# Row tiles taken in turn at the stage borders of a two-block transformer kernel, with five raw and four high weight slots

## The chip, the cores and the metric

The kernel runs on one core of a Trainium2 chip. The metric is the device time of one execution in microseconds (us), the median of several runs. All arithmetic is in float32; a product of two float32 matrices is made of three matmuls on halves, as told below.

## The reference

x is 256 rows (tokens) by 1024. Two different blocks follow each other, each of two layers (DEPTH = 2). Every layer is FFN, token mixer, FFN, each added to the running h. Cut to what matters:

```python
# block 0
for l in range(2):
    h = h + 0.5 * swiglu(rms_norm(h, ffn1_norm[l]), w1[l], w3[l], w2[l])
    h = h + token_mixer(rms_norm(h, mix_norm[l]), ...)     # attention + multiscale pool, gated, @ w_out
    h = h + 0.5 * swiglu(rms_norm(h, ffn2_norm[l]), ...)
h = rms_norm(h, final_norm)
# block 1: the branch's result is normed too, before it is added
for l in range(2):
    h = h + 0.5 * rmsnorm(swiglu_2(rmsnorm(h, ffn1_pre_g[l]), ...), ffn1_post_g[l])
    h = h + rmsnorm(mixer(rmsnorm(h, mix_pre_g[l])), mix_post_g[l])   # scan + retention + attention
    h = h + 0.5 * rmsnorm(swiglu_2(rmsnorm(h, ffn2_pre_g[l]), ...), ffn2_post_g[l])
# rms_norm(x, g) = x * rsqrt(mean(x*x over the row) + 1e-6) * g
```

The hidden width of an FFN is 2816. Twelve stages in all: f1, m, f2 in each of four layers.

## The kernel before

**Tiles.** The 256 rows are two row tiles of 128 (row 0 and row 1, `r` in the code). h lies in SBUF by rows. At the entry of a stage TensorE transposes h, 16 tiles of 128x128, into PSUM banks `work`; ScalarE reads them with the gain as scale and writes the high part `xt_hi` (rounded to the fp32r type), and VectorE writes the low part `xt_lo`. The factor 1/rms of a row is not applied there: it is a number for each row, and is multiplied in behind the first product (the silu and the hidden product of an FFN read `rs`). So the matmuls of a stage can start before the norm is known.

**Weights.** All weights are read once, in units of 128x2048 (1 MB): SyncE (SP) asks for a unit (`load`, two DMAs of 512 KB into `raw`), ScalarE copies it to `w_hi` (`split`, L889), VectorE subtracts to `w_lo` (`split`, L1151), and TensorE multiplies x_hi by w_hi, x_hi by w_lo, and x_lo by w_hi (`product`, L521). A unit takes 24 matmuls, 12 for each row tile. raw, w_hi and w_lo have three slots each, and unit u lies in slot u mod 3. A load waits for `unit_split`: that VectorE is through with the raw slot three units before. ScalarE's copy waits for the load and for `unit_used`: that TensorE is through with the slot.

**An FFN** runs in 11 steps of 256 hidden columns (`steps`). A step has two gate/up units (u, u+1; 4 of the 8 k tiles each) and one down unit (u+4). Its products go to `work[2]` and `work[3]`; silu on ScalarE (L940) and the hidden product on VectorE (L1193) follow, then four transposes (`turn_hidden`), the halves `yt_hi` (ScalarE L945) and `yt_lo` (VectorE L1199), and the down product into `acc`. The gate/up products of step j+1 stand on TensorE before the down product of step j, so the chain of silu and transposes lies beside matmuls, apart from the last step, behind whose gate/up products nothing but its own down product is left.

**What sets the order.** Each engine has its own program, written out by hand, and waits on semaphores whose counts are computed by `Table`s. The steps and the layers are hardware loops (`Fori`). At a border between stages, TensorE ends the last product for both rows; VectorE adds the result to h in four pieces. In block 0 that is one operation for each piece (L1225 behind an FFN). In block 1 it is a norm first (`add_normed`): scale by the post gain from PSUM (L1236), squares on ScalarE (`squares_out`, L914), mean on VectorE (L1172, L1175), the power -1/2 on GpSimd (`power`, L488), and the addition (L1243). Then `turn_h` transposes all 16 tiles, xt_hi (L898) and xt_lo (L1162) follow in four pairs of pieces that hold both rows, and the first chunk (two units, 48 matmuls) begins. On ScalarE the order is: xt_hi of both rows, squares of h, split of unit u+2, split of u+3. On VectorE: xt_lo of both rows, mean, split of u+2 and more.

**SP's order at the border.** Units u and u+1 of the next stage, then `small`: in block 1 (and for f1) it waits for `h_ready`, all four pieces of h, then loads the post gain (and the pre gains), since the buffers of these are in use until then; only then unit u+2.

**Start and end.** x is loaded into `field` and added into h by VectorE (L1144). TensorE's first matmul makes a table of relative biases; behind its first two copies ScalarE issues a DMA that writes this table 128 times into a scratch tensor in DRAM (L922, 3 MB), which block 1 reads later with another stride. At the end one DMA writes all of h (L476).

Of the kernel before, what the change touches and what calls it, by code (L numbers as in the profile page):

```python
# [18 lines left out]
ALU = mybir.AluOpType  # L19
# [4 lines left out]
ds = bass.ds  # L24
# [3 lines left out]
SLOTS = 3  # L28
# [4 lines left out]
class Table:  # L33


    def __init__(self, n, uses):
        self.n, self.at, self.total, k = n, {}, [0] * n, 0
        for name, count in uses:
            for i in range(count):
                self.total[k % n] += 1  # L40
                self.at[name, i] = (k % n, self.total[k % n])
                k += 1
# [5 lines left out]
def tables(block, steps):  # L48

    if block == 0:  # L50
        mix_units = 21
        mix_work = [("turn_m", 4), ("pool", 2), ("qkT", 4), ("scores0", 8), ("probsT0", 8), ("mixp", 2), ("turn_o", 2),
                    ("turn_y", 4)]
        splits = [("turn_m", 4), ("mixp", 2), ("turn_o", 2), ("turn_y", 4)]
        chunks = [("q", 1), ("kv", 1), ("p", 1), ("gate", 3), ("pv0", 1), ("gate_b", 1), ("br_a", 2), ("br_p", 2)]
        norms = ["f1", "m", "f2"]
    else:
        mix_units = 57
        mix_work = [("turn_m", 4), ("rqkT", 4), ("decay", 4), ("ret", 4), ("turn_r", 4), ("qkT", 6),
                    ("scores0", 8), ("probsT0", 8), ("scores1", 8), ("probsT1", 8), ("turn_o", 4),  # L60
                    ("xbcT", 6), ("xsT", 4), ("cb", 2), ("acs", 1), ("seg", 16), ("turn_s", 4), ("turn_y", 4)]
        splits = [("turn_m", 4), ("turn_r", 4), ("turn_o", 4), ("turn_s", 4), ("turn_y", 4)]
        chunks = [("rqk", 2), ("rv", 2), ("gate_r", 2), ("rg", 2), ("aq", 2), ("akv", 1), ("br_r", 2),
                  ("gate_a0", 1), ("pv0", 1), ("gate_a1", 1), ("pv1", 1), ("br_a", 2),
                  ("xbc", 3), ("dt", 1), ("z", 2), ("gate_s", 2), ("ys", 2), ("br_s", 2)]
        norms = ["f1", "p1", "m", "s", "pm", "f2", "p2"]
    return dict(
        units=Table(SLOTS, [("all", 6 * steps + mix_units)]),
        work=Table(4, [("turn_f1", 4)] + mix_work + [("turn_f2", 4)]),
        split=Table(1, [("turn_f1", 4)] + splits + [("turn_f2", 4)]),  # L70
        chunks=Table(2, chunks),
        norms=Table(1, [(n, 1) for n in norms]),
    )


def build(nc, a):
# [7 lines left out]
    T = [tables(b, steps) for b in range(2)]  # L84
# [7 lines left out]
    with ExitStack() as ctx:  # L92
# [7 lines left out]
        raw = sb("raw", [P, SLOTS, UNIT])  # L100
        w_hi = sb("w_hi", [P, SLOTS, UNIT], F32R)
        w_lo = sb("w_lo", [P, SLOTS, UNIT], F32R)
# [16 lines left out]
        ms = sb("ms", [P, 2])  # L119
# [64 lines left out]
        raw_loaded = [sem(f"raw_loaded{s}") for s in range(SLOTS)]  # L184
# [7 lines left out]
        x_loaded = sem("x_loaded")  # L192
# [29 lines left out]
        h_ready = sem("h_ready")  # L222
        squared = sem("squared")
# [7 lines left out]
        pair_added = sem("pair_added")  # L231
# [5 lines left out]
        def count(kind, block, l, name, i=0):  # L237

            slot, k = T[block][kind].use(name, i)
            before = sum(T[b][kind].total[slot] for b in range(block)) * depth  # L240
            return slot, l * T[block][kind].total[slot] + (before + k)

        def unit_count(block, l, pos):

            slot, per, first = pos % SLOTS, T[block]["units"].total, T[0]["units"].total
            return slot, l * per[slot] + ((first[slot] * depth if block else 0) + pos // SLOTS + 1)

        def used_count(block, l, pos, r=1, j=0):

            slot, n = unit_count(block, l, pos)  # L250
            return slot, (n + j) * 2 + (r + 1)

        STAGES = 3

        def h_count(block, l, stage):

            return l * (4 * STAGES) + (4 + (4 * STAGES * depth + 4 if block else 0) + 4 * stage)

        def stage_of(block, name):
            return {"f1": 0, "m": 1, "f2": 2}[name]  # L260

        def norm_count(block, l, name):

            return count("norms", block, l, name)[1] + (1 if block else 0)

        def ffn_count(block, l, name, per):

            return l * (2 * per) + per * ((2 * depth if block else 0) + (name == "f2"))

        first_unit = {(b, "f1"): 0 for b in range(2)}  # L270
        for b in range(2):
            n = sum(T[b]["units"].total)
            first_unit[b, "m"] = 3 * steps
            first_unit[b, "f2"] = n - 3 * steps
            assert n % SLOTS == 0 and first_unit[b, "f2"] % SLOTS == 0
# [6 lines left out]
        def events(block, l, per, k):  # L282

            return l * per[block] + ((per[0] * depth if block else 0) + k)
# [15 lines left out]
        def _(sp):  # L300
            def load(block, l, pos, parts, j=0):

                slot, n = unit_count(block, l, pos)
                n = n + j
                sp.wait_ge(unit_split[slot], n)
                for dst, src in parts(raw[:, slot, :]):
# [1440 lines left out]
```

## Time and profile before

| | before |
|---|---|
| median of 3 runs | 2836.59 us (2836.15 to 2836.85) |
| span of the profiled execution | 2832.0 us |
| TensorE (PE) busy | 2651.5 us, 94% |
| VectorE (DVE) busy | 1551.1 us, 55% |
| ScalarE (ACT) busy | 1225.4 us, 43% |
| GpSimd (POOL) busy | 22.2 us, 1% |

The profiled execution is told by its span only; the 4.6 us between span and median lie around the program. TensorE is busy for 94% of the span, so its idle time, and the stretches in which its granted clock is low, are where time could be. The other engines and the DMA queues matter where TensorE waits for them. In the lines of a timeline, the number in brackets is the idle time of that engine before the instruction, followed by what ended it.

### The profile page before, as it was taken

What the parts mean: (1) busy time and instruction counts of PE and PEld (TensorE: products, weight loads), DVE (VectorE), ACT (ScalarE), POOL (GpSimd) and SP (SyncE); (2) the same over time, 40 slices, a digit from 0 to 9 for tenths busy, and PEclk for the clock granted to TensorE, in tenths of its full rate; (3) what the DMA queues carried; (4) which work ended last, traced back from release to release, by engine and by line L of the source; (5) the groups of instructions that cost most, each with busy time, mean ns of one, the idle gap of its engine ahead of it and who ended that gap; (6) DMA issues with size and microseconds to landing.
All of it is one profiled execution on the core that took longest, in us unless ns stands there. A gap on an engine that the chain in (4) does not pass through costs nothing.

```text
span 2832.0 us, 34364 instructions
## 1 busy us (share of the span) xinstructions
PE 2651.5 (94%) x12238; PEld 2207.2 (78%) x12238; DVE 1551.1 (55%) x1700; ACT 1225.4 (43%) x1431; POOL 22.2 (1%) x28
## 2 busy tenths in 40 slices
PE   6999899999999998999998998898999998998898
PEld 5888778878787787787877877787887877877786
DVE  3555654554565545445556585555445556585544
ACT  4444444444453444444444453444444444453443
POOL 0000000000000000000000000000000000000000
PEclk9999999999999999999999998999999999998999
DMA  9564345555644455655552431563654552441554
GB/s 227 180 228 163 117 151 186 170 179 188 205 149 132 165 190 177 209 189 169 187 168 75 150 134 60 186 192 130 207 188 167 188 169 75 150 134 60 186 190 136
DMA packets 311801, 460.58 MB, mean 163 GB/s; under 512 B 18144, under 2 KB 209936, under 8 KB 311440
## 3 DMA queue, kind: packets, MB, share of 16 engines
q1 hardware_dynamic: 309632, 456.05, 49.0%
q10 hardware_dynamic: 2064, 3.15, 0.9%
q8 instruction: 64, 1.05, 0.2%
q14 instruction: 41, 0.34, 0.0%
HBM read 454.94 MB, written 4.19 MB: 162 GB/s over the span
## 4 chain that ended last, share of the span: by engine, by line
issue 99%; POOL 1%; DVE 0%; DVEq 0%; POOLq 0%
POOL sm L496 0%; POOL rs L488 0%; POOL rp L488 0%; DVE h L1243 0%; DVEq L92 0%; POOLq L487 0%; POOLq L491 0%; POOL minus_half L482 0%; POOLq L495 0%; DVEq L1658 0%; POOLq L488 0%; DVEq L1240 0%; POOLq L1739 0%
## 5 line engine op out<-in xcount | busy, mean ns | idle before, releaser
L1151 DVE TENSOR_TENSOR w_lo<-raw,w_hi 128x2048 fp32r<-128x2048 f32 x422 | 966.5, 2291 | 823.6 <-ACT w_hi L889 823.1
L889 ACT CAST w_hi<-raw 128x2048 fp32r<-128x2048 f32 x422 | 804.6, 1908 | 647.8 <-PE acc L521 325.0
L521 PE MATMUL work<-w_hi,xt_hi 128*128 128x512 f32 x1408 | 562.1, 399 | 27.2 <-DVE xt_lo L1162 27.2
L521 PE MATMUL work<-w_hi,xt_lo 128*128 128x512 f32 x1408 | 553.7, 393 | 0.0
L521 PE MATMUL work<-w_lo,xt_hi 128*128 128x512 f32 x1408 | 552.9, 393 | 0.0
L521 PE MATMUL acc<-w_hi,yt_hi 128*128 128x512 f32 x1088 | 433.4, 398 | 29.9 <-DVE yt_lo L1162 18.3
L521 PE MATMUL acc<-w_lo,yt_hi 128*128 128x512 f32 x1088 | 429.7, 395 | 0.0
L521 PE MATMUL acc<-w_hi,yt_lo 128*128 128x512 f32 x1088 | 429.0, 394 | 0.0
L521 PE MATMUL acc<-w_hi,xt_hi 128*128 128x512 f32 (+2 forms) x896 | 346.7, 387 | 5.3 <-DVE field L1263 4.2
L521 PE MATMUL acc<-w_lo,xt_hi 128*128 128x512 f32 (+2 forms) x896 | 343.2, 383 | 0.0
L521 PE MATMUL acc<-w_hi,xt_lo 128*128 128x512 f32 (+2 forms) x896 | 343.1, 383 | 0.0
L521 PEld LDWEIGHTS work<-w_hi,xt_hi 128*128 128x128 f32 x1408 | 267.7, 190 | 82.9 <-DVE xt_lo L1162 29.7
L521 PEld LDWEIGHTS work<-w_hi,xt_lo 128*128 128x128 f32 x1408 | 267.0, 190 | 57.6
L521 PEld LDWEIGHTS work<-w_lo,xt_hi 128*128 128x128 f32 x1408 | 268.0, 190 | 53.8
L521 PEld LDWEIGHTS acc<-w_hi,yt_hi 128*128 128x128 f32 x1088 | 208.5, 192 | 78.2 <-DVE yt_lo L1162 20.5
L521 PEld LDWEIGHTS acc<-w_hi,yt_lo 128*128 128x128 f32 x1088 | 208.0, 191 | 44.3
L521 PEld LDWEIGHTS acc<-w_lo,yt_hi 128*128 128x128 f32 x1088 | 208.7, 192 | 42.9
L521 PEld LDWEIGHTS acc<-w_hi,xt_hi 128*128 128x128 f32 x896 | 173.5, 194 | 37.8 <-DVE field L1263 4.5
L521 PEld LDWEIGHTS acc<-w_hi,xt_lo 128*128 128x128 f32 x896 | 173.0, 193 | 32.5
L521 PEld LDWEIGHTS acc<-w_lo,xt_hi 128*128 128x128 f32 x896 | 173.4, 194 | 31.6
L940 ACT ACTIVATE field<-work,rs 128x256 f32<-128x256 f32 x176 | 83.3, 475 | 247.5 <-PE work L521 247.4
L945 ACT CAST yt_hi<-work 128x512 fp32r<-128x512 f32 x88 | 51.7, 587 | 296.6 <-PE work L529 296.6
(155 smaller groups left out, 1670.4 us busy)
## 6 DMA issues: line engine op xcount, KB each, us to landing
raw<-ffn_w_dram SPq DMA_DIRECT2D x264, 512.0 KB, 4.1
raw<-w_in_dram SPq DMA_DIRECT2D x204, 512.0 KB, 4.4
raw<-w_ffn_in_dram SPq DMA_DIRECT2D x180, 512.0 KB, 4.6
raw<-w_ffn_out_dram SPq DMA_DIRECT2D x88, 512.0 KB, 4.1
raw<-w_branch_dram SPq DMA_DIRECT2D x48, 512.0 KB, 4.7
raw<-w_out_dram SPq DMA_DIRECT2D x32, 512.0 KB, 4.5
bias<-b_gate_dram SPq DMA_DIRECT2D x10, 512.0 KB, 7.7
raw<-w_branch_attn_dram SPq DMA_DIRECT2D x8, 512.0 KB, 4.2
```

Of the source, the lines that this page charges most:

```text
L521: last = nc.tensor.matmul(out, x[:, kt, k], y[:, slot, w], start=start and n == 0, stop=stop and n == 2)
L889: nc.scalar.copy(w_hi[:, slot, :], raw[:, slot, :]).then_inc(hi_split[slot], 1)
L940: nc.scalar.activation(act_gate[:, r, :], work[2 + r][:, 0:NARROW], ACT.Silu, scale=rs[:, r:r + 1]).then_inc(silu_ready, 1)
L945: nc.scalar.copy(yt_hi[:, 0:2, :], work[0][:, :].rearrange("p (t n) -> p t n", t=2)) \
L1151: nc.vector.tensor_tensor(w_lo[:, slot, :], raw[:, slot, :], w_hi[:, slot, :].bitcast(F32), ALU.subtract).then_inc(unit_split[slot], 1)
```

## The change

- **Slots.** `raw` and `w_lo` have five slots and share their memory (w_lo is written over raw in place), `w_hi` has four. A load no longer waits for `unit_split` of the unit three before, but for `unit_used` of the unit five before.
- **Borders.** Every step of the border is done for row 0 first and then for row 1: the end of the last product, the post norm (`square_out`, `scale_out`, `add_normed` by row), `turn_h(stage, r)`, the pieces of xt_hi and xt_lo (128x128 and 128x256), the squares. Row 0 of the next stage is transposed inside the last product of row 1; row 1 is transposed inside row 0's part of the first chunk (`first_chunk`), which now does 24 matmuls for row 0 and then 24 for row 1. The split of u+2 stands on ScalarE behind row 0's xt_hi and ahead of row 1's; on VectorE behind all of the additions and row 0's xt_lo, and ahead of row 1's xt_lo.
- **Norm factor.** The mean of an entry's norm is made by the squares' scale, and epsilon and the power are both done on GpSimd for each row (`row_scale`), not on VectorE and GpSimd.
- **FFN end.** The last step's transposes and halves are made by row (`turn_hidden_row`, `hidden_row`, in `yt[2:4]`), and stand beside the down product of the step before, which is held back for that.
- **Start.** x is loaded straight into h by row; the table's matmul moves behind the first step's first products, and with it the write to scratch behind the first hidden tile's copy.
- **End.** h is written by row, two DMAs.
- **Small ones.** Three units of mixer 2 (20, 21 and 40) are split only as wide as they are. All loops are unrolled.

```diff
-SLOTS = 3
+SLOTS = 4
+RAWS = 5
...
+        w_lo = nc.alloc_sbuf_tensor_at("w_lo", [P, RAWS, UNIT], F32R, offset=nc.sbuf_base - RAWS * UNIT * 4)
...
+            def load(pos, parts):
+
+                at, _ = raw_count(pos)
+                if pos >= RAWS:
+                    slot, n = used_count(pos - RAWS)
+                    sp.wait_ge(unit_used[slot], n)
...
             def small(block, l, name):
 
-                if block or name == "f1":
-                    sp.wait_ge(h_ready, h_count(block, l, stage_of(block, name)))
+                stage = number[block, l, name]
+                if stage and (block or name == "f1"):
+                    sp.wait_ge(h_ready, h_count(stage))
...
+            def first_chunk(stage, pos, out, early=lambda: None):
+
+                for r in range(2):
+                    for q in range(2):
+                        slot, n = unit_count(pos + q)
+                        pe.wait_ge(unit_split[slot], n + 1)
+                        for t in range(4):
+                            kt = 4 * q + t
+                            if r == 0 and kt == 6:
+                                turn_h(stage, 1)
+                            if kt % 2 == 0:
+                                pe.wait_ge(xt_ready, turn_count(stage, r, kt // 2))
+                            last = product(xt_hi, xt_lo, kt, r, pos + q, t * 512, 512, out(r), kt == 0, kt == kd - 1)
+                        last.then_inc(unit_used[slot], 1)
...
+                turn_hidden_row(steps - 1, 0)
+                down(u + 4 + 3 * j, j, 0)
+                turn_hidden_row(steps - 1, 1)
+                down(u + 3 * steps - 1, steps - 1, 0, 2, end=True)
+                down(u + 4 + 3 * j, j, 1)
...
+                if not early and stage + 1 < len(stages):
+                    turn_h(stage + 1, 0)
+                down_part(u + 3 * steps - 1, 1, 1, 2, end=True).then_inc(unit_used[slot], 1)
...
+                turn_hi_rows(stage, 0, (2, 3))
+                split(u + 2)
+                square_row(0, 4)
+                turn_hi_rows(stage, 1, range(4))
+                square_row(1, 4)
+                split(u + 3)
...
+                elif end == "post":
+                    dve.wait_ge(post_loaded, 16 * (stage - len(stages) // 2) + 16)
+                    scale_out(stage - 1, 0, 0, by)
+                    add_normed(stage - 1, 0, by)
+                    turn_lo_rows(stage, 0, (0, 1))
+                    scale_out(stage - 1, 1, 0, by)
+                    turn_lo_rows(stage, 0, (2, 3))
+                    add_normed(stage - 1, 1, by)
...
+                split(u + 2)
+                turn_lo_rows(stage, 1, range(4))
+                split(u + 3)
```

ScalarE, block 1, from the mixer to f2. Before, behind the squares of the mixer's result, all pieces of xt_hi stood together:

```order
601 L914 ACTIVATE field,sq<-acc 128x512 [waits post_scaled]
603 L898 ACTIVATE xt_hi<-work,vec 128x256 [waits work_filled3]
606 L898 ACTIVATE xt_hi<-work,vec 128x256 [waits work_filled0]
608 L898 ACTIVATE xt_hi<-work,vec 128x256 [waits work_filled1]
610 L898 ACTIVATE xt_hi<-work,vec 128x256 [waits work_filled2]
612 L905 ACTIVATE field,sq<-h 128x1024 x2
613 L889 CAST w_hi<-raw 128x2048 [waits unit_used2,raw_loaded2]
```

The same place now; rows 744 to 751 are xt_hi of row 1:

```order
740 L1070 ACTIVATE xt_hi<-acc,vec 128x128 [waits h_turned]
741 L1070 ACTIVATE xt_hi<-acc,vec 128x128
742 L1024 CAST w_hi<-raw 128x2048 [waits unit_used2,raw_loaded1]
743 L1046 ACTIVATE field,sq<-h 128x1024
744 L1070 ACTIVATE xt_hi<-work,vec 128x128 [waits h_turned]
751 L1070 ACTIVATE xt_hi<-acc,vec 128x128
752 L1046 ACTIVATE field,sq<-h 128x1024
753 L1024 CAST w_hi<-raw 128x2048 [waits unit_used3,raw_loaded2]
```

The cast of unit u+2 moved from behind both rows' pieces to between row 0's and row 1's.

SP at the same place. Before:

```order
458 L307 DMA raw<-w_ffn_in_dram 128x4x256 [waits unit_split0]
460 L307 DMA raw<-w_ffn_in_dram 128x4x256 [waits unit_split1]
463 L341 ISA [waits h_ready]
464 L341 DMA vec<-gain_dram 128x8
465 L345 DMA post<-ffn_post_g_dram 128x1024
468 L307 ISA [waits unit_split2]
469 L307 DMA raw<-w_ffn_in_dram 128x4x256
```

Now:

```order
554 L366 DMA raw<-w_ffn_in_dram 128x4x256 [waits unit_used3]
556 L366 DMA raw<-w_ffn_in_dram 128x4x256 [waits unit_used0]
558 L398 DMA vec<-gain_dram 128x8 [waits h_ready]
559 L401 DMA post<-ffn_post_g_dram 128x1024
560 L366 DMA raw<-w_ffn_in_dram 128x4x256 [waits unit_used1]
562 L366 DMA raw<-w_ffn_in_dram 128x4x256 [waits unit_used2]
```

What the loads of weights wait for changed; that u+2 is asked for behind the wait for h did not.

ScalarE at the start of the program. Before, the write to scratch stood behind the first two casts:

```order
2 L889 CAST w_hi<-raw 128x2048 x2
3 L922 DMA scratch_dram<-field 2048x1x384
4 L1120 UNCONDITIONAL_BRANCH
5 L1120 ISA
6 L895 ISA
7 L898 ACT_TABLE_LOAD
8 L898 ACTIVATE xt_hi<-work,vec 128x256 x4
```

Now it stands behind the first hidden tile's copy, with the casts of four more units ahead of it:

```order
11 L1113 ACT_TABLE_LOAD
12 L1113 ACTIVATE field<-work,rs 128x256
13 L1024 CAST w_hi<-raw 128x2048
14 L1113 ACTIVATE field<-work,rs 128x256
15 L1024 CAST w_hi<-raw 128x2048
16 L1119 CAST yt_hi<-work 128x512
17 L1138 DMA scratch_dram<-field 2048x1x384
18 L1024 CAST w_hi<-raw 128x2048
19 L1113 ACTIVATE field<-work,rs 128x256 x2
```

The 3 MB write moved from before the first products to the first FFN step.

## Rows read from the trace of the kernel before

**Rows 1.** The page, its first part: busy time, share, instructions.

```profile
PE 2651.5 (94%) x12238; PEld 2207.2 (78%) x12238; DVE 1551.1 (55%) x1700; ACT 1225.4 (43%) x1431; POOL 22.2 (1%) x28
```

**Rows 2.** Windows; columns: us, busy by engine, PEclk, DMA share, GB/s.

```profile
660.00:680.00 20.00, 20.00 (x93) 16.60 (x92) 9.23 (x8) 9.44 (x8) 0.00 (x0) 1.00 0.61 192
60.70:63.30 2.60, 2.60 (x8) 2.07 (x7) 2.02 (x2) 2.27 (x2) 0.00 (x0) 0.50 0.96 313
24.60:28.60 4.00, 4.00 (x10) 3.13 (x11) 1.59 (x2) 2.55 (x3) 0.70 (x1) 1.00 0.92 130
```

**Rows 3.** Waits of PE: us in total, times, longest us.

```profile
PE work L521 <- DVE xt_lo L1162: 27.2, 8, 10.1
PE work L529 <- DVE h L1243: 24.7, 5, 5.0
...
PE work L529 <- DVE field L1193: 15.0, 9, 3.9
PE acc L521 <- DVE yt_lo L1199: 11.2, 8, 1.4
...
PE work L529 <- DVE h L1668: 6.1, 1, 6.1
...
PE work L529 <- DVE h L1225: 2.4, 3, 0.9
```

**Rows 4.** Timeline at the start: start, us, engine, line, operation, [idle before <-releaser].

```profile
13.89 1.90 ACT L889 CAST w_hi<-raw 128x2048 fp32r<-128x2048 f32 x1 [0.98 <-DMA raw<-ffn_w_dram]
...
15.82 2.29 DVE L1151 TENSOR_TENSOR w_lo<-raw,w_hi 128x2048 fp32r<-128x2048 f32 x1 [0.58 <-ACT w_hi L889]
...
18.04 0.68 ACTq L922 DMA_DIRECT2D scratch_dram<-field  x1
...
24.51 0.76 PE L521 MATMUL work<-w_hi,xt_hi 128*128 128x512 f32 x1 [10.11 <-DVE xt_lo L1162]
```

**Rows 5.** DMA queues, 30 to 42 us (packets, MB, share); the write's landing time.

```profile
q10 hardware_dynamic: 755, 1.16, 88.2%
q1 hardware_dynamic: 45, 0.14, 2.9%
...
scratch_dram<-field ACTq DMA_DIRECT2D x1, 3072.0 KB, 35.3
```

**Rows 6.** Timeline, ACT, 50 to 60 us.

```profile
54.83 1.90 ACT L889 CAST w_hi<-raw 128x2048 fp32r<-128x2048 f32 x1 [12.79 <-DMA raw<-ffn_w_dram]
...
57.90 1.90 ACT L889 CAST w_hi<-raw 128x2048 fp32r<-128x2048 f32 x1 [0.43 <-DMA raw<-ffn_w_dram]
```

**Rows 7.** Timeline, block 1, from the mixer to f2 of layer 0.

```profile
1775.22 2.74 DVE L1243 SCALAR_TENSOR_TENSOR h<-field,rp,h 128x512 f32<-128x512 f32 x4 [0.91 <-POOL rp L488]
...
1776.69 3.55 PE L529 MATMUL work<-ident,h 128*128 128x128 f32 x16 [4.93 <-DVE h L1243]
...
1778.59 3.43 DVE L1162 SCALAR_TENSOR_TENSOR xt_lo<-work,vec,xt_hi 128x256 fp32r<-128x256 f32 x8 [0.63 <-ACT xt_hi L898]
...
1787.38 1.91 ACT L889 CAST w_hi<-raw 128x2048 fp32r<-128x2048 f32 x1 [4.19 <-DMA raw<-w_ffn_in_dram]
```

**Rows 8.** Timeline, block 1, from f1 to the mixer of layer 0.

```profile
1327.05 2.74 DVE L1243 SCALAR_TENSOR_TENSOR h<-field,rp,h 128x512 f32<-128x512 f32 x4 [0.92 <-POOL rp L488]
...
1337.36 1.91 ACT L889 CAST w_hi<-raw 128x2048 fp32r<-128x2048 f32 x1 [2.22 <-DMA raw<-w_in_dram]
```

**Rows 9.** Timeline, block 0: f1 to the mixer, and layer 0 to layer 1.

```profile
221.35 1.97 PE L529 MATMUL work<-ident,h 128*128 128x128 f32 x16 [0.78 <-DVE h L1225]
...
573.38 1.29 DVE L1225 SCALAR_TENSOR_TENSOR h<-acc,h 128x512 f32<-128x512 f32 x2 [1.22 <-PE acc L521]
...
581.61 1.91 ACT L889 CAST w_hi<-raw 128x2048 fp32r<-128x2048 f32 x1 [1.61 <-DMA raw<-ffn_w_dram]
```

**Rows 10.** Timeline, the end of the program.

```profile
2821.04 0.39 PE L521 MATMUL acc<-w_hi,yt_lo 128*128 128x512 f32 x1
...
2824.88 2.74 DVE L1243 SCALAR_TENSOR_TENSOR h<-field,rp,h 128x512 f32<-128x512 f32 x4 [0.91 <-POOL rp L488]
```

More of the change, by code:

```diff
@@ L271, in build, with unit_count, width, raw_count @@
[L271 to L275, printed above, removed]
+            return T[kind].use((block, l, name), i)
+        def unit_count(pos):
+            return pos % SLOTS, pos // SLOTS + 1
+        def width(pos):
+            return short.get(pos, UNIT)
+        def raw_count(pos):
+            return pos % RAWS, pos // RAWS + 1
@@ new lines, in ffn, with gate_up_rows @@
+                steps_before = ffn_count(block, l, name, steps + 1)
+                def gate_up_rows(pos, j, q, r):
+                    slot, n = unit_count(pos + q)
+                    pe.wait_ge(unit_split[slot], n + 1)
+                    if q == 0:
+                        pe.wait_ge(hidden_ready, hidden_before + (j * 2 + (r + 1)))
+                    for t in range(4):
+                        kt = 4 * q + t
+                        last = product(xt_hi, xt_lo, kt, r, pos + q, t * 512, 512, work[2 + r][:, :],
+                                       kt == 0, kt == kd - 1)
+                    last.then_inc(unit_used[slot], 1)
@@ L928, in ffn, with enter @@
+            def enter(stage, end=None):
+                block, l, name = stages[stage]
+                u = first_unit[block, l, name]
+                if end == "post":
+                    square_out(stage - 1, u - 1, 0)
+                elif end == "final":
+                    act.wait_ge(h_added, 2)
+                    square_row(0, 0)
                 if name == "f1":
                     act.wait_ge(gain1_loaded, l * 16 + (16 + 16 * depth * block))
-                turn_hi(block, l, "turn_" + name, kd, xt_hi, 0, [gain(name) + t for t in range(kd)])
@@ L1219, in ffn @@
+                n = u + 3 * steps
+                hidden_halves(steps - 2)
+                split(n - 1)
+                hidden(steps - 1, 0)
+                split(n)
+                hidden(steps - 1, 1)
+                hidden_row(0)
+                split(n + 1)
+                hidden_row(1)
+                if stage + 1 < len(stages):
+                    enter(stage + 1, "post" if block else "final" if stages[stage + 1][0] else "add")
                 else:
+                    dve.wait_ge(post_loaded, 16 * (stage + 1 - len(stages) // 2) + 16)
```

864 lines of the change are left out of this document (488 added, 376 removed).

## The prediction

> **What bounds the kernel now.** I read the page first: TensorE is busy 2651.5 of 2832.0 us [rows 1], so the time is TensorE's own work plus the roughly 180 us in which it stands. A stretch inside an FFN stage says where it does not stand: 20.00 of 20 us busy, over one turn of the loop and into the next [rows 2]. So neither loop branches nor weights cost anything there, and unrolling the loops (and more weight slots) can give nothing in those stretches: I cost the unrolling at 0. Then the view of who waits for whom, PE alone [rows 3]. Six lines of it belong to the borders between stages and to the start: xt_lo of the first matmul 27.2, h of the post norm 24.7, the first hidden tile 15.0, the hidden halves of the last step 11.2, h of the final norm 6.1, h of block 0 2.4: 86.6 us. Of these the start holds 10.1 and 3.9 (the longest of their lines, before the matmul at 24.51 [rows 4] and near 60 us), so the borders and last steps have 72.6. The rest of the idle time lies inside the mixers, whose order the change leaves alone.
>
> Idle time also costs clock. At full clock a matmul takes 0.227 us: 93 instructions in 20 us, five of them short transposes, so 20/88 [rows 2]. Behind the idle 3.9 near 60 us the granted clock is 0.50, the 1.2 GHz level against 2.4: some seven matmuls at 0.43, 1.4 us too long (2.60 us hold 8 starts, two of them cut by the edges [rows 2]). Behind the 10.1 of the start ten take 4.00, though the clock's record says 1.00 there: at least 1.7, I take 2.0 [rows 2]. At the six normed borders the 16 transposes take some 3.55 us [rows 7] where a short wait leaves them at 1.97 [rows 9]: 6 x 1.6 = 9.6. With 1.4 at five more places (7.0) the borders cost 72.6 + 16.6 = **89.2 us** before.
>
> **What the change takes away there.** Row tile 0 is transposed inside the last products of row tile 1, and the first chunk runs all of row 0 (24 matmuls of 0.227, 5.4 us), then all of row 1. The hidden halves of the last step now lie behind a down product of 12 matmuls (2.7 us) that is already ready; the 1.40 they cost each time (11.2 us, 8 times, [rows 3]) goes. At the two f1-to-m and the two m-to-f2 borders of block 0 nothing else is late: adding one row of h takes two DVE pieces of 0.64 (1.29 for two, [rows 9]), TensorE has 2.7 us in hand, and raw units were requested earlier. There I take all idle as gone.
>
> **What the change leaves in the way.** The weight queue (SP) asks for units u and u+1 of a stage, then waits until all four quarters of h are ready (for the post gain it loads next), and only then asks for u+2. That is unchanged. But ScalarE now has the split of u+2, which waits for that load, *ahead* of the xt_hi pieces of row 1, and VectorE has it ahead of xt_lo of row 1. Before, all 16 transposed tiles came first, and the whole first chunk (48 matmuls, 10.9 us) hid the load. Seven borders have this wait: the entry of f1 in layer 1 of block 0, and all six of block 1.
>
> How long from h to the split? Block 1, m to f2: h ends at 1775.22 + 2.74 = 1777.96, the cast of u+2 starts at 1787.38, held by the DMA: 9.4 us [rows 7]. Into m: 1329.79 to 1337.36, 7.6 us [rows 8]. Block 0: 574.67 to 581.61, 6.9 us [rows 9]. The same three units go out in one burst in both kernels, so I keep these. Behind it: cast 1.9, w_lo 2.29 (square and xt_hi of row 1 lie beside it), first xt_lo pair 0.6 (3.43 for eight of 256 columns [rows 7]; half as wide is 0.22 to 0.43 each, I take 0.3): 4.8 us.
>
> When is h of row 1 complete? Before, the idle time starts at 1776.69 - 4.93 = 1771.76 and h is done 6.2 us later, for both rows [rows 7]. For row 1 alone one square, one scaling and two h pieces fewer stand in the chain (about -2.1), but VectorE and ScalarE first finish the last two xt pairs of row 0 (+1.2): 5.3 us behind the last product, bounds 4 and 6.5. In that time TensorE has row 0's chunk and 8 transposes, 6.3 us. So TensorE idles:
> f2 and f1 of block 1 (three borders): 5.3 + 9.4 + 4.8 - 6.3 = 13.2, with 0.4 for h of row 0: 13.6 each, 40.8;
> m of block 1 (two): 5.3 + 7.6 + 4.8 - 6.3 + 0.4 = 11.8 each, 23.6;
> the final norm's border: two norms in a row, 13.6 + 2.5 = 16.1;
> f1 of layer 1, block 0: h is done after 2.2: 2.2 + 6.9 + 4.8 - 6.3 = 7.6.
> Sum 88.1, and seven spells of low clock at 1.8 (between 1.4 and 2.0), 12.6: **100.7 us after against 89.2 before, +11.5**.
>
> **Start.** Now x goes straight into h, and the table matmul no longer stands first. The second cast starts at 13.89 and takes 1.90 [rows 4]; with one more DMA ahead, 16.3; w_lo 2.29, first xt_lo 0.6: first matmul at 19.2 for 24.51, -5.3. The wait of 3.9 and the low clock behind it go (-5.3). So TensorE is 10.6 ahead, were it not for the 3 MB table write. Before it was issued at 18.04 [rows 4], landed 35.3 us later, and stopped the weights: from 30 to 42 us its queue q10 moved 1.16 MB and the weights' q1 0.14 [rows 5], ScalarE stood 12.79 for a unit, which came at 54.83, the next at 57.90 [rows 6]: 1.5 and 4.5 behind the end of the write. Much of that was hidden by the late start. Now the write goes out only after the first hidden tile, near 41 us, and ends near 75 (its queue meets less company, -1 to -2). Units 8 and 9 are asked for at 44.6 and 50, when units 3 and 4 are used, so unit 9 lands near 79; ScalarE has both splits ahead of step 2's silu. Cast 1.9, two silus, two hidden pieces: TensorE goes on at 82 where it could at 67. Stall 15 (bounds 0 and 17), clock 1.8: start **-10.6 + 16.8 = +6.2**.
>
> If the two queues shared each engine's time evenly, the loads would keep half their rate and both units would land before 60: no stall. The Trainium skill, DMA: Bandwidth & Descriptors, "Queues, rings and completion order", says each DMA engine serves its queue rows round-robin, packet by packet; by that rule the loads would not be starved, and the total would be the 2833 of the third rival below. Rows 5 speak against an even share here.
>
> **Tail.** The last product to the end of the span is now 10.6 us; h of both rows is out at 2824.88 + 2.74 = 2827.62 and one DMA of 1 MB follows [rows 10]. Row 0 leaves early; for row 1 alone 3.5 and 3.3: 6.8. **-3.8**.
>
> **Small ones.** Norm factors on GpSimd run beside the first chunk; narrower splits for units 20, 21 and 40 save VectorE and ScalarE some 5 us per mixer where they wait for TensorE anyway: 0, bounds -4 and +2. A unit is now asked for when the fifth before it is used, one unit (5.44 us) ahead of its cast; the burst-free landing is near 5 us, so ScalarE may wait by tenths inside the mixers: 0, up to +8.
>
> **Sum.** 11.5 + 6.2 - 3.8 = +13.9. The profiled execution's span is 2832.0, and 4.6 us lie around it up to the median of 2836.6; I leave those as they are: 2836.6 + 13.9 = **2850 us**.
>
> **Rivals.**
> (1) *The wait for u+2 doesn't bind*, because the load lands inside row 0's chunk. Then the seven borders keep only the chain to h of row 1 and the w_lo ahead of xt_lo, about 2 us each: 100.7 falls to 14 to 18, time 2767. It needs a landing within 2 us of the request; rows 7 to 9 show 6.9 to 9.4. 5%.
> (2) *Partly*: h comes at the lower bound and the burst lands 2 us earlier, as less else is in flight: -3.3 at seven borders, 2827. 10%.
> (3) *The table write doesn't stall step 2*: -16.8, time 2833, no change. For: a load of 256 long rows may pass between the write's packets. Against: rows 5 and 6. 16%.
> (4) *ScalarE becomes the late one in the mixers*, by raw units that land after their high slot is free: 156 units, and wherever the wait exceeds the slack the softmax and scan chains move. Decides if a unit takes over 5.4 us from request to landing, while 7 to 9 were seen in bursts: +10 to +20, time 2865. 9%.
> My forecast, all as summed: 60%.
>
> **How the numbers follow.** About 0.2%, 5.7 us, is what can be told from no change. Slower: forecast and rival 4, less the part of the forecast's spread that falls under 2842: 0.64. Same: rival 3 and that part: 0.21. Faster: rivals 1 and 2: 0.15. Range: 2826 takes in rival 3 and most of 2; 2866 takes in the upper bounds of the chain (7 x 1.2), the stall (+2) and rival 4's lower half.
>
> **What would show it.** PE's gaps before row 1's first xt matmul of 11 to 14 us at six borders, each ended by xt_lo, with ScalarE's cast held by a raw DMA just before; a gap of some 15 us near 67 to 82; no gap at the mixers' entry and exit in block 0; FFN stretches still 20.00 of 20. Wrong if those gaps are under 5 us, or if casts inside the mixers wait for DMA by more than a few tenths.

## The result, and the profile after

The changed kernel took 2841.09 us (median of 19 runs) where the kernel before took 2834.04 beside it; the ratio is 1.0021, with a 95% interval of 1.0014 to 1.0028: slower by 6 us (4 to 8). The forecast of 2850 from 2836.6 was +13.4. The direction was right and the range held the time, but the size was more than twice what was measured. One of the changed kernel's 19 runs took 3582.69 us at a granted clock of 0.70 and is left out of the ratio. The two profiled executions differ by 7.0 us: spans of 2832.0 and 2839.0. (A run's time is its span plus 1.8 us, 2840.82 for the 2839.0 here. So of the 4.6 us that were put around the program ahead of the prediction, 2.8 are something else: the profiled execution of the kernel before was that much shorter than its median.)

The page of the kernel after, its first part (compare [rows 1]):

```profile
span 2839.0 us, 30036 instructions
...
PE 2639.4 (93%) x12238; PEld 2196.0 (77%) x12238; DVE 1544.9 (54%) x1787; ACT 1223.6 (43%) x1530; POOL 48.2 (2%) x71
```

TensorE's busy time is 12 us less and the span 7 us more, so TensorE idles 19 us more. Who it waits for (after, PE, us in total, times, longest):

```profile
PE work L586 <- DVE xt_lo L1355: 63.8, 7, 11.9
PE acc L586 <- DVE yt_lo L1342: 20.9, 8, 4.0
PE acc L586 <- DVE xt_lo L1355: 20.0, 2, 10.4
PE work L593 <- DVE field L1453: 17.4, 1, 17.4
...
PE work L669 <- DVE field L1453: 4.2, 1, 4.2
```

Against [rows 3]: the wait for h (24.7, 6.1, 2.4) and that for the last step's hidden halves (11.2) are gone, and the wait for xt_lo went from 28.3 (27.2 in `work`, 1.1 in `acc`) to 83.8 us, 10.5 of it at the start. The 20.9 for yt_lo is another wait: all eight lie inside the mixers, where the kernel before has 18.3. Two single waits stand out, of 17.4 and of 4.2 us. The longer waits for xt_lo and the one of 17.4 were forecast, that of 4.2 was not. Inside an FFN stage nothing changed (a window of after, as in [rows 2]):

```profile
660.00:680.00 20.00, 20.00 (x91) 16.55 (x91) 10.65 (x7) 8.00 (x7) 0.00 (x0) 1.00 0.65 207
```

**Border from the mixer to f2, block 1, after** (timeline; compare [rows 7]):

```profile
1783.87 1.42 DVE L1396 SCALAR_TENSOR_TENSOR h<-field,rp,h 128x512 f32<-128x512 f32 x2
...
1785.69 0.43 SPq L401 DMA_DIRECT2D post<-ffn_post_g_dram  x1
...
1786.17 2.16 SPq L366 DMA_DIRECT2D raw<-w_ffn_in_dram  x4
...
1786.99 0.40 PE L586 MATMUL work<-w_hi,xt_lo 128*128 128x512 f32 x1
...
1793.27 1.90 ACT L1024 CAST w_hi<-raw 128x2048 fp32r<-128x2048 f32 x1 [10.82 <-DMA raw<-w_ffn_in_dram]
...
1795.20 2.29 DVE L1331 TENSOR_TENSOR w_lo<-raw,w_hi 128x2048 fp32r<-128x2048 f32 x1 [9.91 <-ACT w_hi L1024]
...
1797.41 1.12 DVE L1355 SCALAR_TENSOR_TENSOR xt_lo<-work,vec,xt_hi 128x128 fp32r<-128x128 f32 x4
...
1798.16 0.77 PE L586 MATMUL work<-w_hi,xt_hi 128*128 128x512 f32 x1 [10.77 <-DVE xt_lo L1355]
```

Read it from the bottom. TensorE waits 10.8 us for xt_lo of row 1. VectorE has the first pieces of it 0.75 us after it begins, but has w_lo of unit u+2 ahead of it, which waits for ScalarE's cast, which waited 10.82 us for a DMA that SP asked for at 1786.17, behind its wait for h (done at 1785.29). The view of waits names only the last link, xt_lo; the cause is four links up.

A table over all stages helps to find the rest. Each entry is worked out from the start times of the products (10176 in each trace): at a border, from the start of the 24th-last product of one stage to that of the 49th of the next, and inside a stage the remainder, each less 0.227 us (a product at full clock) for every product in it. What is left is idle time, low clock, and the short transposes.

| us beyond the products | before | after |
|---|---|---|
| start (first 48 products) | 28.5 | 22.5 |
| rest of the first FFN | 12.0 | 26.9 |
| block 0: into m and f2, four borders | 23.9 | 8.4 |
| block 0: layer 0 to layer 1 | 9.2 | 11.4 |
| block 0 to block 1 (final norm) | 15.3 | 17.8 |
| block 1: into m, two | 18.5 | 27.7 |
| block 1: f2 and f1, three | 43.1 | 46.2 |
| inside the last FFN of block 0 | 6.2 | 13.1 |
| inside the six other FFNs | 37.5 | 31.6 |
| inside the four mixers | 317.0 | 317.1 |
| tail | 10.8 | 6.3 |

### The profile page after: what moved, and what is told of

Its sections match the earlier page's. It is cut to its first block, busy times and chain, and to the rows that moved or that the text cites. A ratio compares the mean times of both kernels' runs of the same rounds, so it can differ in the third digit from the quotient of the medians.

```text
span 2839.0 us, 30036 instructions
## 1 busy us (share of the span) xinstructions
PE 2639.4 (93%) x12238; PEld 2196.0 (77%) x12238; DVE 1544.9 (54%) x1787; ACT 1223.6 (43%) x1530; POOL 48.2 (2%) x71
## 3 DMA queue, kind: packets, MB, share of 16 engines
HBM read 452.84 MB, written 4.19 MB: 161 GB/s over the span
## 4 chain that ended last, share of the span: by engine, by line
PE 85%; DVE 5%; ACT 3%; DMA 3%; issue 2%; SPq 1%; DVEq 0%; POOL 0%; ACTq 0%
PE acc L586 45%; PE work L586 32%; PE work L593 2%; PE acc L797 2%; ACT w_hi L1024 2%; DMA raw<-ffn_w_dram 1%; PE work L781 1%; DMA raw<-w_ffn_in_dram 1%; DVE w_lo L1331 1%; PE work L993 1%; DVE xt_lo L1355 1%; SPq L366 0%; DVE field L1519 0%; DMA raw<-w_in_dram 0%; PE work L810 0%
## 5 line engine op out<-in xcount | busy, mean ns | idle before, releaser
L1331 DVE TENSOR_TENSOR w_lo<-raw,w_hi 128x2048 fp32r<-128x2048 f32 (+1 forms) x420 | 953.5, 2272 | 879.8 <-ACT w_hi L1024 879.4
L1024 ACT CAST w_hi<-raw 128x2048 fp32r<-128x2048 f32 (+1 forms) x420 | 794.6, 1893 | 693.8 <-PE acc L586 294.6
L586 PE MATMUL acc<-w_hi,yt_hi 128*128 128x512 f32 x1088 | 435.6, 400 | 21.6 <-DVE yt_lo L1342 20.9
L586 PEld LDWEIGHTS work<-w_hi,xt_hi 128*128 128x128 f32 x1408 | 268.0, 190 | 125.5 <-issue 72.6
L586 PEld LDWEIGHTS acc<-w_hi,xt_hi 128*128 128x128 f32 x896 | 173.9, 194 | 57.1 <-issue 20.9
```

The lines of the kernel that those rows point to most:

```text
L586: last = nc.tensor.matmul(out, x[:, kt, k], y, start=start and n == 0, stop=stop and n == 2)
L1024: nc.scalar.copy(w_hi[:, slot, 0:n], raw[:, at, 0:n]).then_inc(hi_split[slot], 1)
L1331: nc.vector.tensor_tensor(w_lo[:, at, 0:n], raw[:, at, 0:n], w_hi[:, slot, 0:n].bitcast(F32), ALU.subtract).then_inc(unit_split[slot], 1)
```

## The experiments

Each kernel was timed beside the kernel before; the numbers are medians, and the ratio is to the kernel before (2834.75 us in the first group of four, 2834.72 in the second, 2835.39 in the last). The theory: the request of u+2, held back by SP's wait for h, is what costs at seven borders, because its split now stands ahead of row 1's xt. Rivals: the chain to h of row 1; the order of the splits by itself; a late request that is dear in any order.

### 1. SP asks first, then waits

```diff
-                small(block, l, name)
                 for j in range(steps - 1):
                     load(u + 3 * j + 2, gate_up(block, name, l, j + 1, 0))
                     load(u + 3 * j + 3, gate_up(block, name, l, j + 1, 4))
+                    if j == 0:
+                        small(block, l, name)
```

(and the same in the mixer of block 1, where `small` moves behind the third and fourth unit)

> The changed kernel with one edit on SP: at all stage entries the wait for h and the loads of the gains stand behind the loads of units u+2 and u+3 instead of ahead of them. Nothing else moves. Theory (the request of u+2 is late, and the split of u+2 ahead of row 1's xt turns that into TensorE idle): the seven gaps of 8 to 12 us before row 1's first product fall to about 3 (h chain, and w_lo of 2.3 ahead of xt_lo), so about 8 each and some low clock: 55 to 65 us less, near 2780. Rival (the chain to h of row 1, post norm by row, is what ends last): the gaps stay above 8 us and the time falls by less than 10.

**2762.23 us, ratio 0.9751 (0.9731 to 0.9770)**: 79 us less than the changed kernel, and 18 below the 2780 expected. The same border in its trace:

```profile
1745.71 1.93 ACT L1026 CAST w_hi<-raw 128x2048 fp32r<-128x2048 f32 x1
...
1747.28 1.41 DVE L1398 SCALAR_TENSOR_TENSOR h<-field,rp,h 128x512 f32<-128x512 f32 x2
...
1748.61 2.28 DVE L1333 TENSOR_TENSOR w_lo<-raw,w_hi 128x2048 fp32r<-128x2048 f32 x1
...
1750.81 1.12 DVE L1357 SCALAR_TENSOR_TENSOR xt_lo<-work,vec,xt_hi 128x128 fp32r<-128x128 f32 x4
...
1751.56 0.47 PE L588 MATMUL work<-w_hi,xt_hi 128*128 128x512 f32 x1 [0.76 <-DVE xt_lo L1357]
```

The cast now ends before h is done, w_lo follows h at once, and TensorE waits 0.76 us where it waited 10.77. I had expected 3: the chain to h of row 1 is 4.6 us and not 5.3, and row 0's products with the transposes fill 6.7 of it and not 6.3. Summed over the eleven borders, TensorE's idle time falls from 76.3 to 8.6 us and the excess at low clock from 15.1 to 3.4, together 79.4, as much as the two spans differ (2839.0 and 2759.7). (A wait is counted here from 0.227 us behind the start of the product before it; the profile has that product's end 0.17 later. By the profile's gaps alone the idle time is 74.5 and 7.0.) Inside the stages two smaller differences cancel: the mixers take 6.2 us less, and the six FFNs 7.0 more, with new waits of 0.9 to 2.1 us for a first hidden tile in block 1. The chain to h of row 1 is refuted as a rival: it is still there, unchanged.

### 2. The split behind row 1's xt, SP as it was

```diff
                 turn_hi_rows(stage, 0, (2, 3))
-                split(u + 2)
                 square_row(0, 4)
                 turn_hi_rows(stage, 1, range(4))
+                split(u + 2)
                 square_row(1, 4)
```

(on VectorE likewise: the split of u+2 behind `turn_lo_rows(stage, 1, range(4))`)

> The changed kernel with the other half undone: ScalarE and VectorE take the split of u+2 behind row 1's xt_hi and xt_lo; SP still waits for h before it asks for u+2. Theory: the load still lands 8 us behind h, but TensorE has row 1's 24 products (5.4 us) to do meanwhile, so each of seven gaps shrinks by about 5.4 and moves behind the first chunk, where it reads as a wait for w_lo: 35 to 40 us less, near 2803. Rival (the h chain): the gap before row 1's first product stays, less than 10 us gained.

**2828.79 us, ratio 0.9979 (0.9968 to 0.9990)**: 12 us less, not 38. The border:

```profile
1791.76 1.90 ACT L1024 CAST w_hi<-raw 128x2048 fp32r<-128x2048 f32 x1 [5.84 <-DMA raw<-w_ffn_in_dram]
...
1796.66 1.28 ACT L1113 ACT_TABLE_LOAD   x1
...
1797.96 0.47 ACT L1113 ACTIVATE field<-work,rs 128x256 f32<-128x256 f32 x1
...
1798.89 0.47 DVE L1453 SCALAR_TENSOR_TENSOR field<-work,rs,field 128x256 f32<-128x256 f32 x1
1799.51 0.77 PE L586 MATMUL work<-w_hi,xt_hi 128*128 128x512 f32 x1 [8.11 <-DVE field L1453]
```

The gap moved behind the first chunk, as expected, but it is a wait for the first hidden tile, not for w_lo: the silu stands behind the splits of both u+2 and u+3 on ScalarE, so it comes 6.2 us after the late cast begins (two casts of 1.90, a square of 1.05 and a table load of 1.28), and the product 1.6 later. The expectation had only the wait for w_lo, which is ready at 1795.98. Undoing the order without the request gives little.

### 3. Both

The two edits together.

> Both edits together: the loads of u+2 and u+3 ahead of the wait for h, and the split of u+2 behind row 1's xt. Theory: nothing but the chain to h of row 1 is left, 5.3 us for which TensorE has 6.3; gaps under 1.5 us, low clock gone: 75 to 85 us less than the changed kernel, near 2760. If the first edit alone gives all, this one is within 5 us of it; by my sum it is 15 to 20 us faster, since w_lo of u+2 (2.3 us) no longer stands ahead of xt_lo.

**2776.65 us, ratio 0.9800 (0.9784 to 0.9816)**: 14 us *slower* than the first edit alone, where 15 to 20 faster was expected by the sum. Its trace:

```profile
1763.80 1.12 DVE L1357 SCALAR_TENSOR_TENSOR xt_lo<-work,vec,xt_hi 128x128 fp32r<-128x128 f32 x4 [0.53 <-ACT xt_hi L1072]
...
1769.99 2.29 DVE L1333 TENSOR_TENSOR w_lo<-raw,w_hi 128x2048 fp32r<-128x2048 f32 x1 [0.55 <-ACT w_hi L1026]
1771.27 0.47 ACT L1115 ACTIVATE field<-work,rs 128x256 f32<-128x256 f32 x1
...
1772.83 0.77 PE L588 MATMUL work<-w_hi,xt_hi 128*128 128x512 f32 x1 [2.01 <-DVE field L1455]
```

No wait before row 1's first product is left, but casts and w_lo of u+2 and u+3 now run one behind the other between row 1's xt and the first silu, and TensorE waits 2.0 us for the hidden tile, at FFN entries of block 0 too. So the early place of the split is right, and is worth 14 us, *if* the unit has been asked for. The change put it there and left the request behind. The rival of the order by itself is answered with this: taking the order back gains 12 us with the late request and loses 14 with the early one.

### 4. The same edit on the kernel before

> The kernel BEFORE with the same edit on SP alone (loads of u+2 and u+3 ahead of the wait for h). Theory: there both rows' xt stood ahead of the split of u+2 and 48 products hid the load, so the late request cost little: only the 1 us by which the first hidden tile's wait is longer in block 1 than in block 0 (2.6 against 1.5), so 0 to 8 us less than before. Rival (the late request is dear by itself, whatever the order of the splits): 50 to 80 us less, as in the changed kernel.

**2832.52 us, ratio 0.9993 (0.9984 to 1.0003)**: no measurable difference, though the edit did what it should, as the border from the mixer to f2 shows:

```profile
1784.82 1.90 ACT L893 CAST w_hi<-raw 128x2048 fp32r<-128x2048 f32 x1
...
1796.12 0.66 PE L533 MATMUL work<-ident,field 128*128 128x128 f32 x4 [1.08 <-DVE field L1197]
```

The cast no longer waits for a DMA (4.19 us in the kernel before), and the wait for the first hidden tile falls from 2.18 to 1.08 us. So the late request was in the old kernel all the time and cost about 1 us at such a border: all xt stood ahead of the split, and 48 products covered the load. This refutes the rival of a request that is dear in any order.

### 5. The table write in eight pieces

```diff
-                    elif stage == 0:
-                        act.wait_ge(table_ready, 2)
-                        act.dma_start(a["scratch"], field[0:16, 5000:5384].unsqueeze(1).broadcast_to([16, P, 3 * P])) \
+                    if stage == 0 and j < 8:
+                        k = slice(j * 16, (j + 1) * 16)
+                        act.dma_start(a["scratch"][:, k, :],
+                                      field[0:16, 5000:5384].unsqueeze(1).broadcast_to([16, 16, 3 * P])) \
```

> The changed kernel with the 3 MB write of the bias table to DRAM cut into eight pieces of 384 KB, one for each of the first eight FFN steps. Theory (one long write starves the weight queue for 33 us): a piece lasts some 4 us and the loads behind it have slack, so the gap of 17 us at 69 us goes, with low clock 15 to 19 us less: near 2823. Rival (the write takes its 33 us from the loads however it is cut, since they share the engines): the loss is only spread, less than 5 us gained, with small gaps in the steps up to 130 us.

The stall that it is about, in the kernel after (timeline of ScalarE, then of TensorE):

```profile
52.77 0.59 ACT L1119 CAST yt_hi<-work 128x512 fp32r<-128x512 f32 x1 [3.61 <-PE work L593]
78.40 1.90 ACT L1024 CAST w_hi<-raw 128x2048 fp32r<-128x2048 f32 x1 [25.05 <-DMA raw<-ffn_w_dram]
81.39 1.90 ACT L1024 CAST w_hi<-raw 128x2048 fp32r<-128x2048 f32 x1 [1.09 <-DMA raw<-ffn_w_dram]
```

```profile
86.45 1.11 PE L593 MATMUL work<-ident,field 128*128 128x128 f32 x4 [17.37 <-DVE field L1453]
```

**2819.43 us, ratio 0.9952 (0.9935 to 0.9968)**: 22 us less than the changed kernel. In the stretch of 42 to 80 us, first the kernel after and then the one with pieces (queue: packets, MB, share; then the write: KB, us to landing):

```profile
q10 hardware_dynamic: 2064, 3.15, 74.4%
...
scratch_dram<-field ACTq DMA_DIRECT2D x1, 3072.0 KB, 35.9
```

```profile
q10 hardware_dynamic: 816, 1.18, 15.7%
...
scratch_dram<-field ACTq DMA_DIRECT2D x2, 384.0 KB, 5.7
```

A piece lands in 5.7 us and the next is asked for 10.6 us after it or later (16.6 and more for all but the first), so no weight unit waits for long: the loads of this stretch land in 4.3 us where they took 12.8 (medians). The rest of the first FFN falls from 26.9 us beyond its products to 7.0: the stall was worth 19.9.

### 6. The same edit on the kernel before, and the unrolling alone

> The kernel BEFORE, unrolled, with the table write cut into eight pieces, one behind each of the first eight FFN steps, and not in one behind the first two casts. Theory: before, the write cost only the wait of 3.9 us near 60 us with its low clock, and 1 us near 38, so 5 to 8 us less than before, where the same edit gave 22 on the changed kernel: the rest of what it cost was hidden by the late start. Rival (the write cost the same in both kernels): 15 to 22 us less.

```diff
-                with sp.Fori(0, steps - 1) as j:
+                for j in range(0, steps - 1):
```

> The kernel BEFORE with all hardware loops unrolled and nothing else. Forecast: 0, within 3 us, since FFN stretches have TensorE busy for 20.00 of 20 us. What it can give lies at the borders, where SP takes 1.39 us from the end of h to the request of u+2 (0.88 in the changed kernel). Rival: register work of the loops is part of every border's chain, 0.5 us each: 5 to 8 us less.

With pieces and unrolled: **2825.49 us, ratio 0.9966 (0.9953 to 0.9979)**. Unrolled alone: **2832.46 us, ratio 0.9997 (0.9987 to 1.0007)**. So the write's one piece cost 7 to 9 us in the old kernel (the intervals leave some 5 either way), and 22 in the new: its move into the first FFN step made it dearer, which is the forecast's second term. The unrolling costs and gives nothing measurable here, though it shortens one thing that comes to matter: at the entries of f2 in block 1, SP takes 0.89 us from the end of h to the request of u+2, and 1.39 with loops. (The spans of the profiled executions of these two are equal, 2826.3 and 2826.4. In them the rest of the first FFN falls from 14.2 to 6.3 us beyond its products, and the mixers, whose work is the same, rise from 311.7 to 318.7; see the end.)

### 7. Block 1's tables later

```diff
-                    for dst, src in ((decay, a["decay"]), (rope2, a["rope2"])):
-                        sp.dma_start(dst, src).then_inc(blk_loaded, 16)
-                    sp.wait_ge(scratch_stored, 16)
-                    sp.dma_start(rel_bias, bass.AP(a["scratch"].tensor, P - 1,
```

(these DMAs now stand behind the down units of steps 1 and 3 of block 1's first FFN)

> The changed kernel with block 1's tables (decay, rotations, and the 2 MB of relative biases) loaded in the second and fourth step of block 1's first FFN, and not ahead of that stage's first weight units. Theory: in the last step of block 0 ScalarE and VectorE now split block 1's first unit ahead of the last hidden tile, and that unit is queued behind these tables: a wait of 4.6 us and what follows it, 7 us in all, which was not in my sum. It goes: 6 to 8 us less than the changed kernel, near 2834. Rival (the wait comes from the halved last step itself): no change; then the tables may even hold up the FFN's units, up to 5 us more.

What it is about, in the kernel after, at the end of block 0:

```profile
1091.41 0.44 SPq L523 DMA_DIRECT2D blk<-scratch_dram  x1
1094.28 4.86 SPq L366 DMA_DIRECT2D raw<-w_ffn_in_dram  x2
```

```profile
1108.11 1.90 ACT L1024 CAST w_hi<-raw 128x2048 fp32r<-128x2048 f32 x1 [7.44 <-DMA raw<-w_ffn_in_dram]
...
1112.25 0.48 DVE L1453 SCALAR_TENSOR_TENSOR field<-work,rs,field 128x256 f32<-128x256 f32 x1
...
1112.78 0.69 PE L669 MATMUL work<-ident,field 128*128 128x128 f32 x2 [4.22 <-DVE field L1453]
```

Block 1's first unit comes behind 2 MB of relative biases, 13.8 us after its request, and both engines have its split ahead of the last hidden tile. **2836.21 us, ratio 1.0007 (0.9998 to 1.0017)**: 5 us less than the changed kernel by the medians; the two intervals just overlap, and the trace has to say where it lies. Inside that FFN the 13.1 us beyond the products fall to 6.1, as expected; 3.3 come back at the border behind it (17.8 to 21.1), where TensorE's waits for h and xt_lo grow from 12.1 to 15.0.

### 8. The three edits together

> The changed kernel with three edits: u+2 and u+3 asked for ahead of the wait for h (79 us less by itself), the table write in eight pieces (22 less), block 1's tables later (7 less). If the three are independent stalls, as theory has it, they add up: near 2735. If the pieces or the tables only push weight loads against the earlier requests, it stays above 2745.

**2740.92 us, ratio 0.9667 (0.9651 to 0.9683)**. The parts, 79, 22 and 5, sum to 106; measured 100, and the intervals of the four ratios, 3 to 6 us either way each, cover the difference. The page of this kernel:

```profile
PE 2621.4 (96%) x12238; PEld 2181.0 (80%) x12238; DVE 1543.8 (56%) x1787; ACT 1221.8 (45%) x1530; POOL 54.0 (2%) x71
```

### 9. Four raw slots

```diff
-RAWS = 5
+RAWS = 4
```

> The three-edit kernel (2741 us) with four raw slots instead of five. A unit is then asked for only when the fourth before it is used, which is when its high slot comes free too, so ScalarE waits for a landing of 4.5 us at each of 420 units and everything behind it in its queue comes that much later. Theory (the fifth slot is what keeps the load off ScalarE's path; rival 4 of the forecast did not come true because of it): FFN steps stay full, as 16.3 us pass before TensorE needs the unit, but hidden tiles come late: 20 to 100 us slower than 2741. Rival (slack is enough): within 5 us.

**2995.8 us, ratio 1.0565 (1.0546 to 1.0583)**: 255 us slower than with five, far above the 100 that I set as the upper end. Who ScalarE waits for:

```profile
ACT w_hi L1025 <- DMA raw<-ffn_w_dram: 446.0, 125, 9.4
ACT w_hi L1025 <- DMA raw<-w_in_dram: 361.0, 87, 14.6
ACT w_hi L1025 <- DMA raw<-w_ffn_in_dram: 316.3, 80, 13.4
```

There are 446 us in 125 waits for one weight tensor, where the five-slot kernel has 82.2 in 23. Most FFNs have 18 us beyond their products for 6 to 9, and the mixers of block 1 162 for 122: the cast stands ahead of silu, softmax and scan work in ScalarE's queue. The direction was right, the size not. The kernel before lived with three slots, since its load waited only for the split of the unit three before; here a load waits for TensorE's last use of the slot.

### 10. The start

```diff
                 load(u + 1, gate_up(block, name, l, 0, 4))
+                if u == 0:
+                    sp.dma_start(field[0:32, 4096:4112], a["rel_bias_2"]).then_inc(consts_loaded, 16)
...
-            split(0)
-            split(1)
             enter(0)
...
                 turn_hi_rows(stage, 0, (2, 3))
+                if stage == 0:
+                    split(0)
+                    split(1)
                 split(u + 2)
```

> The three-edit kernel with two edits at the start: the five small tables are asked for behind the first two weight units instead of ahead of them (five issues of 0.46, 2.3 us), and both halves of x for row 0 stand ahead of the first two splits on ScalarE and VectorE (they were 3.5 us of the way from the first w_lo to the first product). Theory: first product at 13 to 14 us instead of 18.9, so 4 to 6 us less: near 2736. Rival (the second unit's w_lo then is late, TensorE stops behind 12 products): 2 us or less.

**2736.79 us, ratio 0.9657 (0.9637 to 0.9677)**, 4 us less than experiment 8 by the medians, 3 by the ratios, whose intervals overlap; expected were 4 to 6. The first product:

```profile
14.82 0.79 PE L588 MATMUL work<-w_hi,xt_hi 128*128 128x512 f32 x1 [6.68 <-DVE w_lo L1337]
```

It starts 4 us earlier than the 18.86 of the kernel after, and the start takes 19.2 us beyond its products for 22.4 in experiment 8. This kernel has the lowest median of the study, 3.4% below the kernel before and 3.7% below the changed one.

## Why the prediction came out twice too large

**What bounds the kernel, and what the change takes away: right.** The short borders of block 0 went from 23.9 to 8.4 us beyond the products. The last step's wait went: 37.5 to 31.6 for six FFNs, a little under 1 us each in spite of 0.5 of transposes that now fall inside.

**The border term, +11.5, was wrong: it was -6.1.** This is the step that failed. The mechanism is the one that was named (experiments 1 to 4), but both totals were off, in opposite ways.

- *Before* was put at 89.2 us and is 97.5: 65.8 idle at the eleven borders, 20.5 of low clock, 11.2 for the last steps. The idle time was read rightly: by the profile's gaps the borders and last steps have 61.4 + 11.2 = 72.6, the figure of the prediction. But each of some 25 waits costs about 0.17 us more than its gap (experiment 1), some 4 in all, and the low clock is 20.5 and not 16.6. It was 3.4 and 4.4 us, not 1.6, at the two borders into an f1 of block 1: there eight and twelve products run at 0.43 us behind the second idle spell (1.87 and 2.72 us, behind a first of 6.11 and 5.01). At the two borders from the mixer to f2 there are also two spells (4.93 and 1.93) and the products behind them run at 0.23, so that there are two spells does not explain it.
- *After* was put at 100.7 and is 91.4 (76.3 idle, 15.1 low clock). The sum for a border into f2 of block 1 was 5.3 + 9.4 + 4.8 - 6.3 + 0.4 = 13.6. The trace has 4.6 + 8.0 + 4.9 - 6.7 = 10.8. Over the seven borders the waits are 73.3 us by the profile's gaps and were put at 88.1. Four terms share the error: the chain to h of row 1 (5.4 too much), the load from h to the cast (4.5), TensorE's work meanwhile (3.9 too little, 6.7 and not 6.3 at five borders and 8.1 at the final norm), and 0.4 for h of row 0, which appeared only at the final norm as 0.8 us (1.6 too much). From the cast to the product the sum had 0.1 too little each time. The load is the one that could have been foreseen. 9.4 came from [rows 7], and of it SP took 1.39 us from the end of h (1777.96) to the request:

```profile
1779.35 2.34 SPq L307 DMA_DIRECT2D raw<-w_ffn_in_dram  x4
```

The cast came 8.0 later. Now SP takes 0.88 and the cast comes 7.1 later. The 0.5 is the unrolling (experiment 6 has 0.89 with nothing else changed), which the prediction cost at 0 because it gives nothing inside an FFN. I had copied a duration from a kernel in which nobody waited for it, without looking at which part of it was SP's own.

A difference of two large sums takes the error of both: 8.3 too little before and 9.3 too much after make 17.6 us in a forecast of 13.9.

Of the signs that were named, the gaps before row 1 at the six borders are 9.6 to 11.9 us for a forecast of 11 to 14, each ended by xt_lo; the seventh is 7.5 for 7.6.

**The start, +6.2, was +10.3.** The first product was put at 19.2 and came at 18.86. The stall was put at 15 and 1.8 and is worth 19.9 (experiment 5). Units 8 and 9 are the ones that come late, at 78.40 and 81.39, as forecast. The write went out at 42.27 and landed 35.9 us later, near 78 and not 75.

The Trainium skill, DMA: Bandwidth & Descriptors, "Queues, rings and completion order", has a DMA engine serve its queues in turn, a packet at a time. The queues of the kernel after, from 48 to 60 us and from 62 to 76 (packets, MB, share):

```profile
q10 hardware_dynamic: 756, 1.16, 90.3%
```

```profile
q10 hardware_dynamic: 858, 1.31, 84.2%
q1 hardware_dynamic: 881, 0.89, 17.9%
```

In the second stretch the trace agrees: the write's queue and the weights' queue move one packet for one. But a packet of the write is 1.5 KB and takes nearly five times the engines' time of one of the loads, 1.0 KB, so a unit of 1 MB needs some 16 us at this rate. Turns by packet are not even shares of time, and the third rival (2833) did not follow from the page's rule. In the first stretch the weights' queue moved nothing, though unit 8 was asked for at 46.88; why it stood until 60.8 no run here shows.

**The tail, -3.8, was -4.5** (10.8 to 6.3).

**A term that was missing, +7.0**: the split of the *next* stage's first unit now stands ahead of the last hidden tile, in every FFN. I looked at that order for the split of u+2 only. It matters once, where 2 MB of tables are queued ahead of that unit (experiment 7).

Sum: -6.1 + 10.3 - 4.5 + 7.0 = +6.7, for 7.0 between the spans. The errors, -17.6, +4.1, -0.7 and +7.0, cancel in part; that the range held the time is partly luck. Of the rivals, (1), in which the wait does not bind, gave 2767, and that is where experiment 1 ends when the wait is taken away (2762). (4), ScalarE late in the mixers, did not come as a cost: the mixers have 317.1 us for 317.0. Its sign did come, and I had called it one of being wrong: ten casts inside the mixers wait for a DMA, up to 4.3 us, and 27 in all, where the kernel before has none. TensorE lost nothing by them that shows. Experiment 9 shows, on the kernel with the three edits, that the fifth raw slot keeps the cost away: with four, casts wait 546 us for DMAs inside the mixers, and the kernel loses far more than the 10 to 20 of this rival. I gave it 9%.

What stays open: why the low clock follows some idle spells and not others, and why the weights' queue stood from 46.9 to 60.8 us.

## What to carry to other kernels

When an operation moves ahead in one engine's queue, look up who *asks* for its data, and move the request with it; a wait that cost nothing measurable (ratio 0.9993) becomes the bound (79 us) when its cover goes, and the view of waits will name only the last link. Put a number on the old state by the same method, gap by gap, as on the new: the forecast is their difference. A long DMA beside a tight load stream is cheaper in pieces.

## What the runs showed of the hardware

A write of 3 MB that took 35.9 us in one piece goes in eight pieces of 384 KB with 5.7 us each, and beside them the loads go on (they land in 4.3 us, and in 12.8 beside the one piece); nothing else of it had to change. Two queues that move packet for packet shared the engines' time 84 to 18.

The granted clock differs between passes over the same work. A window of the first mixer of block 1 in the kernel before, and in the same kernel unrolled (the work in the two windows is shifted by up to 5 us):

```profile
1340.00:1780.00 440.00, 406.57 (x1942) 344.07 (x1941) 272.37 (x392) 191.15 (x267) 5.00 (x3) 0.93 0.39 128
```

```profile
1340.00:1780.00 440.00, 402.48 (x1952) 339.89 (x1951) 275.06 (x397) 195.76 (x274) 5.70 (x4) 0.94 0.40 132
```

Counted from the same product to the same product (the 49th to the 24th-last), this mixer took 422.7 us before and 417.0 unrolled; the clock's record has 61.3 and 40.8 us at 0.50 in it, and TensorE's idle time is 28.5 and 30.7. It is not the unrolling: the second layer's mixer of the unrolled kernel, in the same execution, took 422.7, with 57.9 at 0.50. The spans differ by 5.7 us (2832.0 and 2826.3) where the medians differ by a ratio of 0.9997. So the 7.0 us between two profiled executions could not have told this change's sign; 19 runs of each could.
